# The matrix-memory layer of a small transformer: dense work spread in equal pieces, transposes one block later

## Chip, cores and metric

The kernel runs on one core of one Trainium2 chip. The metric is the time of one execution on the device, in microseconds (us). The engines are TensorE (PE, matmuls; PEld is its weight load), VectorE (DVE), ScalarE (ACT), GpSimd (POOL) and SyncE (SP, which issues the weight transfers). All data is 32-bit.

## The reference

Two blocks of two layers run on 256 latent and 256 context tokens of width 1024. Each layer has a mixer and a squared-ReLU MLP of width 4096. The change touches one mixer of the four, the "mLSTM" (matrix memory) of the second block's first layer. It has 8 heads, with queries and keys of 64 and values of 128:

```
q, k, v, o, gates = split(u @ w_in)                 # u: normed input, 512 tokens
b = cumsum(log_f);  d = b[t] - b[s] + log_i[s]      # per head and direction, masked to the scan's past
m_t = max(max_s d, inter)
wq = exp(d - m_t) * (q @ k.T)                       # decay weights times scores
h = (wq @ v + carry) / max(|sum(wq) + carry|, exp(-m_t))
hs = h_forward + flip(h_backward)
y = (rms_norm_per_head(hs) * head_norm * sigmoid(o)) @ w_out
```

The kernel writes the chunked recurrence out as one masked product per head: for every tile of 128 queries, exp(decay arguments) times the scores, for both directions, normalised, added, transposed and multiplied with the values.

## The kernel before, in words

Every large product is made of three fast passes (L646 to L648), because each 32-bit operand is split in a rounded high part and a rest: high x high, low x high, high x low. A weight tile of 128 x 2048 comes into `ring` by a transfer from SP, ACT rounds it into `w_h` (L1145, two halves), and DVE subtracts to get `w_l` (L1509, two halves). Both hold two tiles. Each engine has its own queue, written out by hand in the order of the code, and semaphores tie the queues together.

The layer's mixer is in these phases:

- `m_in`: gates, queries, keys and the first quarter of the values. Its last tile has four units, one for each 128 tokens, which DVE copies out of PSUM (L1496).
- `m_gates`: 16 small transposes on PE (L1024) turn the gate rows into columns, and DVE copies them into `tm` (L1955).
- `m_heads`: 32 blocks, b = 4 x head + query tile. In the first two query tiles of a head (latent) a block has 512 keys, in the other two (context) 256. "Long" and "short" blocks are meant by this below.
- `to_h` with `m_out`: four tiles of the output projection. Beside them DVE makes the modulation vectors of a later layer out of streamed weights (L1528, L1530), adds the results to `h` (L1899) and splits the next weights.

One block of `m_heads` goes through the engines so: POOL adds the mask to the decay rows (`args`, L2159); ACT makes the exponentials (`decay`, L1393 and L1395: four for a long block, two for a short one); PE makes the scores (`qk`, L1038); DVE multiplies the two and sums (L1990, twice, called W below), works out the reciprocal (L1995 to L1997); ACT scales the forward part with it (`scale`, L1402); DVE adds the backward part (L2010, called P); PE transposes (`turn`, L1048) into bank 5; ACT copies that out (`turned`, L1409); PE multiplies two such blocks with the values (`values`, L1064). After each head there are copy (`head_out`, L1415), squares (L2166), mean square on PE (`mean_square`, L1072), logarithm, exponent and norm (L1420, L1973, L1427, L1965), rounding (`round_out`, L1431) and rest (`rest_out`, L1580) for the output projection.

The blocks' decay arguments are in three buffers, `mbuf(b)`. `args(b)` overwrites the buffer of block b-3 and so waits until `turn(b-3)` is done. `qk` has two banks, and `qk(b)` waits for W of block b-2.

Among the blocks stands the rest of the input projection, 20 dense units of 24 passes: 12 token-major ones for the values (`tokm`, 256 columns) and 8 feature-major ones for the output gate (`fm`, 512 columns). `dense_slots` puts unit k in block 3k//2, so two blocks of three have one and every third has none. In the code of PE:

```
for b in range(n):
    if b + 2 < n:
        qk(b + 2)
    dense(b)
    turn(b)
    if b % 2 == 0 and b:
        values(b // 2 - 1)
    if b % 4 == 3 and b > 4:
        mean_square(b // 4 - 1)
```

## Time and profile before

| | |
|---|---|
| time before, median of 3 runs | 2445.49 us (2441.13 to 2446.42) |
| the profiled execution, its own time | 2443.79 us |
| its span | 2442.0 us |
| PE busy over the span | 2269.7 us (93%) |
| DVE, ACT, POOL busy | 1679.6, 885.2, 672.5 us |
| `m_heads`, first `qk` to first pass of the output projection | 1418.69 to 1628.90 us |

The profiled execution's time is 1.79 us more than its span, for what lies around the span, and 1.70 us less than the median. "Busy" counts a matmul's modelled duration, at whatever clock it ran. PEclk is TensorE's granted clock as a share of 2.4 GHz, so 0.50 is 1.2 GHz. A number in brackets behind a timeline row is the idle time of that engine before it, and who ended it; "x4" means four instructions merged.

### The profile page before, as it was taken

Reading aid. Unit: us, or ns where it says so; the run is one execution under the profiler, and the core shown is the slowest. Engines: PE = TensorE matmul, PEld = TensorE weight load, DVE = VectorE, ACT = ScalarE, POOL = GpSimd, SP = SyncE. Lnnn points to the kernel's source line nnn. Section 1 sums busy time; section 2 is a strip of 40 time slices with the busy share of each in tenths; the row PEclk is TensorE's granted clock in tenths of the full one; section 3 lists DMA queues with packets and bytes.
Section 4 is the critical chain, followed back from the end, with each engine's and each line's share of the span. In section 5 each row is a group of like instructions: output and inputs, shape, how many; then the busy total and the mean of one; then the engine's idle time right before and its main releaser. Section 6 shows DMA issues by size and latency. Waiting matters only on the chain. (4 is left out here: it accounts for less than half of the span.)

```text
span 2442.0 us, 31167 instructions
## 1 busy us (share of the span) xinstructions
PE 2269.7 (93%) x12408; PEld 1892.2 (77%) x12408; DVE 1679.6 (69%) x2431; ACT 885.2 (36%) x1357; POOL 672.5 (28%) x434
## 2 busy tenths in 40 slices
PE   5999999899999889999988888878999998898998
PEld 5887678688888678899987666656888887657997
DVE  6665658988669955767777845569876775596343
ACT  1323333222333233444433445542223334244444
POOL 3001210233345500113465022212323462002244
PEclk9999999999999989999988989889999999899999
DMA  8422124455555462356655421113655564203652
GB/s 278 153 87 74 47 87 155 138 198 181 189 190 185 141 188 77 114 162 192 216 173 161 146 82 61 52 52 132 212 179 201 190 172 97 69 1 106 189 173 86
DMA packets 268025, 341.14 MB, mean 140 GB/s; under 512 B 31056, under 2 KB 181464, under 8 KB 267624
## 3 DMA queue, kind: packets, MB, share of 16 engines
q1 hardware_dynamic: 266704, 334.92, 42.8%
q10 hardware_dynamic: 1176, 4.23, 0.5%
q8 instruction: 99, 1.62, 0.3%
q14 instruction: 46, 0.38, 0.0%
HBM read 338.04 MB, written 1.08 MB: 139 GB/s over the span
## 5 line engine op out<-in xcount | busy, mean ns | idle before, releaser
L646 PE MATMUL PS<-a_h,w_h 128*128 128x512 f32 (+1 forms) x2808 | 974.9, 347 | 43.8 <-DVE a_l L1689 28.5
L647 PE MATMUL PS<-a_l,w_h 128*128 128x512 f32 (+1 forms) x2808 | 961.8, 343 | 0.0
L648 PE MATMUL PS<-a_h,w_l 128*128 128x512 f32 (+1 forms) x2808 | 961.3, 342 | 0.0
L1509 DVE TENSOR_TENSOR w_l<-ring,w_h 128x1024 fp32r<-128x1024 f32 (+1 forms) x434 | 596.9, 1416 | 257.0 <-ACT w_h L1145 256.3
L646 PEld LDWEIGHTS PS<-a_h,w_h 128*128 128x128 f32 x2808 | 541.2, 193 | 138.0 <-issue 57.4
L1145 ACT ACTIVATE w_h<-ring 128x1024 fp32r<-128x1024 f32 (+1 forms) x434 | 426.7, 1033 | 583.1 <-PE PS L648 529.5
L648 PEld LDWEIGHTS PS<-a_h,w_l 128*128 128x128 f32 x2808 | 540.9, 193 | 59.6
L647 PEld LDWEIGHTS PS<-a_l,w_h 128*128 128x128 f32 x2808 | 541.8, 193 | 56.0
L1530 DVE SCALAR_TENSOR_TENSOR bias<-ring,silu,bias 128x512 f32<-128x512 f32 x532 | 453.3, 906 | 4.2 <-DMA ring<-in_w_mod 0.5
L2076 POOL TENSOR_TENSOR a_l<-hid,a_h 128x2048 fp32r<-128x2048 f32 (+1 forms) x60 | 228.4, 3807 | 241.6 <-ACT a_h L1161 241.6
L2091 POOL TENSOR_TENSOR hid<-hid 128x256 f32<-128x256 f32 (+1 forms) x128 | 157.7, 1233 | 414.8 <-ACT hid L1127 414.8
L1127 ACT ACTIVATE hid<-PS 128x512 f32<-128x512 f32 (+1 forms) x136 | 67.6, 498 | 382.0 <-PE PS L648 381.8
L1553 DVE TENSOR_REDUCE mod<-PS 128x4 f32<-128x512 f32 x76 | 49.5, 684 | 132.6 <-PE PS L714 132.2
L646 PE MATMUL PS<-w_h,a_h 128*128 128x256 f32 x384 | 116.8, 304 | 20.7 <-DVE a_l L1689 20.5
L2120 POOL TENSOR_TENSOR bias<-windows,aux 128x256 f32<-128x256 f32 x32 | 29.3, 938 | 311.6 <-DVE nmax L1794 163.9
L647 PE MATMUL PS<-w_l,a_h 128*128 128x256 f32 x384 | 113.2, 295 | 0.0
L648 PE MATMUL PS<-w_h,a_l 128*128 128x256 f32 x384 | 113.0, 294 | 0.0
L1127 ACT ACTIVATE big<-PS 128x256 f32<-128x256 f32 (+1 forms) x90 | 41.7, 464 | 192.0 <-PE PS L648 191.9
L646 PE MATMUL PS<-m_h,w_h 128*128 128x512 f32 (+1 forms) x320 | 108.3, 338 | 1.0 <-DVE m_l L1765 1.0
L648 PE MATMUL PS<-m_h,w_l 128*128 128x512 f32 (+1 forms) x320 | 107.5, 336 | 0.0
L647 PE MATMUL PS<-m_l,w_h 128*128 128x512 f32 (+1 forms) x320 | 107.5, 336 | 0.0
L646 PEld LDWEIGHTS PS<-w_h,a_h 128*128 128x128 f32 x384 | 78.4, 204 | 33.6 <-issue 28.8
(181 smaller groups left out, 2379.6 us busy)
## 6 DMA issues: line engine op xcount, KB each, us to landing
ring<-in_w_ff SPq DMA_DIRECT2D x64, 1024.0 KB, 5.7
ring<-in_ffn_w SPq DMA_DIRECT2D x64, 1024.0 KB, 5.5
ring<-in_w_mod SPq DMA_DIRECT2D x48, 1024.0 KB, 5.2
ring<-in_ada_w SPq DMA_DIRECT2D x48, 1024.0 KB, 5.2
ring<-in_w_in SPq DMA_DIRECT2D x42, 1024.0 KB, 5.3
ring<-in_mlstm_w_in SPq DMA_DIRECT2D x12, 1024.0 KB, 5.6
ring<-in_w_o SPq DMA_DIRECT2D x8, 1024.0 KB, 5.0
ring<-in_w_attn_out SPq DMA_DIRECT2D x4, 1024.0 KB, 5.6
```

The lines of the kernel that those rows point to most:

```text
L646: nc.tensor.matmul(out, stat[0], mov[0], start=start, stop=False, **kw)
L647: nc.tensor.matmul(out, stat[0], mov[1], start=False, stop=False, **kw)
L648: return nc.tensor.matmul(out, stat[1], mov[0], start=False, stop=stop, **kw)
L1127: nc.scalar.activation(out, PS[0:m, bank_of[u], src_cols], func, **kw).then_inc(s_free[bank_of[u]], 1)
L1145: nc.scalar.activation(w_h[:, n % 2, c], raw[:, c], ACT.Copy).then_inc(s_wh, 1)
L1509: V.tensor_tensor(w_l[:, n % 2, c], ring[:, split_raw[n] % SLOTS, c], w_h[:, n % 2, c].bitcast(F32), ALU.subtract).then_inc(s_wl, 1)
L1530: ins = V.scalar_tensor_tensor(out=acc[:, v, :], in0=w[:, k, :], scalar=sc, in1=acc[:, v, :], op0=ALU.mult, op1=ALU.add)
L1553: ins = V.tensor_reduce(sums[:, :, v], PS[:, 6 + v, :].rearrange("p (c n) -> p c n", n=P), AX_X, ALU.add)
L2076: nc.gpsimd.tensor_tensor(lo, hid[:, 4 * (g % 8):4 * (g % 8) + 4, 0:cols], hi.bitcast(F32), ALU.subtract).then_inc(s_xl, 1)
L2091: nc.gpsimd.tensor_tensor(x, x, x, ALU.mult).then_inc(s_ff, 1)
L2120: ins = nc.gpsimd.tensor_tensor(bias[:, hh % 2, c].rearrange("p (i c) -> p i c", i=4), shifted, aux[:, A_MASK + LAT * q:A_MASK + LAT * q + ...
```

## The change

The order of work of the matrix-memory layer is written anew in the queues of all engines:

- **Pieces.** A dense unit of 512 columns is cut in halves, so that there are 28 pieces: 16 halves of 12 passes and 12 token-major units of 24. `piece(b)` puts one in each block but 8, 17, 26 and 31.
- **Transposes.** PE does `turn(b-1)` at the end of its turn through the loop for block b, and so `values` and the last steps shift by one turn. ACT does `turned(b-1)` right behind `scale(b)` and ahead of `decay(b+2)`.
- **Weights.** Rounding and splitting are done by halves, one in each of two blocks. The tile that follows the seventh, `m_out`'s second, is no longer prepared in `m_heads`.
- **Gates.** The 16 transposes of the gate rows stand behind the second unit of `m_in`'s last tile, in bank 5, and DVE copies them behind its second copy.
- **Output projection.** Its first tile goes over k for both units together, and the last head's mean square stands in it, behind k = 5.

```
-            return {3 * k // 2: unit for k, unit in enumerate(units)}
+        def piece(b):
+            p = b - (b // 9)
+            return (p // 4, p % 4) if b % 9 < 8 and p < 28 else None
+        TILE_ENDS = {-1: -1, 0: 3, 1: 7, 2: 12, 3: 16, 4: 21, 5: 25}
+        def tile_to_prepare(b, since):
+            return next((i + 2 for i, end in TILE_ENDS.items() if end + since == b), None)
...
@@ PE, output projection
+                        if ph["src"] == "m" and i == 0:
+                            for ks in (range(0, 6), range(6, 8)):
+                                if ks[0]:
+                                    mean_square(MH - 1)
+                                for k in ks:
...
@@ PE, m_in
                             if i == 5:
                                 tokm(st, u + j, w, j)
+                                if j == 1:
+                                    gate_columns()
...
@@ PE, m_heads
-                    for b in range(n):
+                    for b in range(n + 1):
                         if b + 2 < n:
                             qk(b + 2)
-                        dense(b)
-                        turn(b)
-                        if b % 2 == 0 and b:
-                            values(b // 2 - 1)
+                        if b < n:
+                            dense(b)
+                        if b % 2 and b > 2:
+                            values((b - 3) // 2)
+                        if b:
+                            turn(b - 1)
                         if b % 4 == 3 and b > 4:
                             mean_square(b // 4 - 1)
                     values(2 * MH - 1)
-                    mean_square(MH - 1)
...
@@ ACT, m_heads
-                    round_w(ph["s"] + 1)
                     decay(0)
                     decay(1)
                     for b in range(n):
-                        if b % 4 == 0 and b >= 8:
-                            log_variance(b // 4 - 2)
                         scale(b)
+                        if b:
+                            turned(b - 1)
                         if b + 2 < n:
                             decay(b + 2)
...
+                        if qt == 2 and hh >= 1:
+                            head_out(hh - 1)
+                        if qt == 2 and hh >= 2:
+                            norm_and_gate(hh - 2)
+                        for i in range(2):
+                            t = tile_to_prepare(b, 1 + i)
+                            if t is not None:
+                                round_half(ph["s"] + t, i)
+                        if qt == 0 and hh >= 2:
+                            log_variance(hh - 2)
+                        if qt == 0 and hh >= 3:
+                            round_out(hh - 3)
+                        if piece(b) is not None and piece(b)[0] % 2 == 0 and piece(b)[1] % 2:
+                            output_gate(piece(b)[0], piece(b)[1] // 2)
+                    turned(n - 1)
...
@@ DVE, m_heads
                         dve.wait_ge(s_scaled, b + 1)
                         V.scalar_tensor_tensor(out=x0, in0=x1, scalar=rc[:, 1:2], in1=x0, op0=ALU.mult, op1=ALU.add
                                                ).then_inc(s_P, 1)
+                        for i in range(2):
+                            t = tile_to_prepare(b, 2 + i)
+                            if t is not None:
+                                split_half(ph["s"] + t, i)
+                        if qt == 3 and hh >= 2:
+                            normed(hh - 2)
+                        if qt == 1 and hh >= 3:
+                            rest_out(hh - 3)
```

Two places show how it moves instructions. The first is ACT's queue in the middle of `m_heads`. L1402 is `scale`, L1409 `turned`, L1393 `decay` and L1415 `head_out`. Before, from a copy of transposes on:

```order
604 L1409 ACTIVATE work<-PS 128x4x128 [waits m_pv_done,m_transposed]
605 L1402 ACTIVATE work<-work,den 128x512 [waits m_denominator_ready]
606 L1393 ACTIVATE work<-work,tm 128x256 [waits m_decay_args]
607 L1393 ACTIVATE work<-work,tm 128x256
608 L1415 ACTIVATE hid<-PS 128x512 [waits m_pv_done]
609 L1409 ACTIVATE work<-PS 128x4x128 [waits m_pv_done,m_transposed]
```

Of the change, one turn through the same loop. Here L1439 is `scale`, L1446 `turned`, L1430 and L1432 `decay`, L1452 `head_out`, L1464 the exponential of the norm and L1182 half a weight tile's rounding:

```order
663 L1439 ACTIVATE work<-work,den 128x256 [waits m_denominator_ready]
664 L1446 ACTIVATE work<-PS 128x4x128 [waits m_pv_done,m_transposed]
665 L1430 ACTIVATE work<-work,tm 128x256 [waits m_decay_args,m_decay_rows_loaded_0]
666 L1432 ACTIVATE work<-work,tm 128x256
667 L1430 ACTIVATE work<-work,tm 128x256
668 L1432 ACTIVATE work<-work,tm 128x256
669 L1203 DMA bias<-decay_rows 128x1024 [waits m_decay_args]
670 L1452 ACTIVATE hid<-PS 128x512 [waits m_pv_done]
671 L1464 ACTIVATE aux<-aux 128x512 [waits m_exponent_ready]
672 L1182 ACTIVATE w_h<-ring 128x1024 [waits unit_done,weights_loaded_0]
673 L1439 ACTIVATE work<-work,den 128x256 [waits m_denominator_ready]
```

The copy of the transposes, which stood last in a block, now stands between the block's `scale` and its `decay`, and everything else of the block stands between `decay` and the next `scale`.

The second place is PE's queue where the heads end. "windows,unit" is a mean square, "work,big" the values, "m_h,w_h" the output projection. Before, from the last transposes on:

```order
7310 L1048 MATMUL PS<-ident,work 128x128 [waits m_probsT_ready,m_probs_ready]
7311 L1048 MATMUL PS<-ident,work 128x128
7312 L1072 MATMUL PS<-windows,unit 128x512 [waits m_squares]
7313 L1064 MATMUL PS<-work,big 128x256 [waits m_probsT_ready]
7314 L1064 MATMUL PS<-work,big 128x256
7315 L1072 MATMUL PS<-windows,unit 128x512 [waits m_squares]
7316 L646 MATMUL PS<-m_h,w_h 128x512 [waits input_split,bank_evacuated_2,weights_split]
```

Of the change, the end of the 36 passes that now stand ahead of the last mean square, which is L731 here:

```order
7348 L648 MATMUL PS<-m_h,w_h 128x512
7349 L649 MATMUL PS<-m_l,w_h 128x512
7350 L650 MATMUL PS<-m_h,w_l 128x512
7351 L731 MATMUL PS<-windows,unit 128x512 [waits m_squares]
7352 L648 MATMUL PS<-m_h,w_h 128x512 [waits input_split]
```

The last mean square has moved from the front of the output projection to behind six of eight k of its first tile.

## Rows read from the trace of the kernel before

**Rows 1.** Busy us of PE, PEld, DVE, ACT, POOL, then granted clock, in two stretches.

```profile
1418.00:1629.00 211.00, 173.18 (x753) 125.50 (x753) 113.89 (x307) 110.21 (x220) 51.17 (x40) 0.85 0.15 50
1633.00:1679.00 46.00, 42.04 (x194) 34.81 (x193) 44.71 (x62) 8.07 (x9) 17.18 (x13) 1.00 0.53 173
```

**Rows 2.** Waits from 1418 to 1629 us: who, for whom, total, times, longest.

```profile
PE PS L1048 <- DVE work L2010: 31.7, 10, 5.9
```

**Rows 3.** Timeline of PE alone, blocks 5 and 6, at full clock.

```profile
1460.16 0.60 PE L1048 MATMUL PS<-ident,work 128*128 128x128 f32 x4
1460.60 1.03 PE L1064 MATMUL PS<-work,big 128*128 128x256 f32 x4
1461.56 0.70 PE L1038 MATMUL PS<-big 64*128 64x256 f32 x2
...
1463.52 1.12 PE L1038 MATMUL PS<-big 64*128 64x512 f32 x2
...
1464.58 0.39 PE L646 MATMUL PS<-w_h,a_h 128*128 128x256 f32 x1
...
1467.56 0.38 PE L1048 MATMUL PS<-ident,work 128*128 128x128 f32 x2
1467.78 1.89 PE L1064 MATMUL PS<-work,big 128*128 128x256 f32 x8
```

**Rows 4.** Timeline of POOL, ACT and DVE at the same place.

```profile
1460.85 1.27 POOL L2159 TENSOR_TENSOR work<-bias,aux 128x512 f32<-128x512 f32 x1 [2.85 <-PE PS L1048]
1461.29 0.71 ACT L1402 ACTIVATE work<-work,den 128x512 f32<-128x512 f32 x1
1462.04 0.75 DVE L2010 SCALAR_TENSOR_TENSOR work<-work,den 128x512 f32<-128x512 f32 x1 [1.25 <-ACT work L1402]
1462.15 0.91 ACT L1393 ACTIVATE work<-work,tm 128x256 f32<-128x256 f32 x2
1462.71 0.41 DVE L1990 CUSTOM_DVE_ANT_0 work<-work,PS 128x256 f32<-128x256 f32 x1
```

**Rows 5.** Groups by line and shape, 1418 to 1629 us: count, busy, mean ns, idle.

```profile
L1509 DVE TENSOR_TENSOR w_l<-ring,w_h 128x1024 fp32r<-128x1024 f32 x16 | 20.6, 1329 | 26.4 <-ACT w_h L1145 26.3
L1145 ACT ACTIVATE w_h<-ring 128x1024 fp32r<-128x1024 f32 x15 | 15.0, 1046 | 0.0
```

**Rows 6.** Granted clock (third from the right) in short stretches.

```profile
1464.00:1468.00 4.00, 4.00 (x30) 3.40 (x29) 3.00 (x11) 2.27 (x7) 1.92 (x2) 1.00 0.33 128
1504.00:1508.00 4.00, 4.00 (x19) 3.82 (x19) 2.46 (x8) 1.40 (x3) 0.00 (x0) 0.50 0.24 94
1316.00:1318.00 2.00, 2.00 (x11) 2.00 (x11) 1.97 (x4) 0.00 (x0) 2.00 (x1) 0.50 0.97 333
```

**Rows 7.** Timeline of PE: waits that ended shortly before those stretches.

```profile
1501.65 0.44 PE L1048 MATMUL PS<-ident,work 128*128 128x128 f32 x2 [3.54 <-DVE work L2010]
1314.28 1.42 PE L714 MATMUL PS<-ident,bias 128*128 128x128 f32 x8 [2.10 <-DVE bias L1530]
```

**Rows 8.** Timeline where the heads begin.

```profile
1416.43 1.15 PE L1024 MATMUL PS<-ident,work 8*128 8x8 f32 x16
1422.85 0.69 DVE L1990 CUSTOM_DVE_ANT_0 work<-work,PS 128x512 f32<-128x512 f32 x1 [0.74 <-ACT work L1395]
1424.21 1.22 PE L1038 MATMUL PS<-big 64*128 64x256 f32 x2 [3.57 <-DVE den L1990]
```

**Rows 9.** Timeline where they end and the output projection begins.

```profile
1623.36 0.63 PE L1048 MATMUL PS<-ident,work 128*128 128x128 f32 x2
1628.35 1.12 PE L1072 MATMUL PS<-windows,unit 128*128 128x512 f32 x2 [1.80 <-POOL windows L2166]
1633.08 0.69 DVE L1580 TENSOR_TENSOR m_l<-hid,m_h 128x512 fp32r<-128x512 f32 x1 [0.70 <-ACT m_h L1431]
1640.43 0.88 DVE L1899 SCALAR_TENSOR_TENSOR h<-PS,mod,h 128x256 f32<-128x256 f32 x2 [1.11 <-PE PS L648]
1651.11 1.03 PE L714 MATMUL PS<-ident,bias 128*128 128x128 f32 x8
```

More of the change, by code:

```diff
@@ L1006, in _, with gate_columns @@
                 elif kind == "m_in":
+                    def gate_columns():
+                        pe.wait_ge(s_gr, 1)
+                        out = PS[:, 5, :].rearrange("p (w t g n) -> p w t g n", w=2, t=4, g=2, n=32)
+                        for what in range(2):
+                            for d in range(2):
+                                src = G[:, 2 * d + 1, :] if what == 0 else Bc[:, d, :]
+                                for tt in range(4):
+                                    mm = nc.tensor.transpose(out[:, what, tt, d, 0:MH], src[:, P * tt:P * tt + P],
+                                                             ident[0:MH, 0:MH])
+                        mm.then_inc(s_cols, 1)
                     first_tile(ph["steps"][0], ph["x"] - KC, False, gate_view)
@@ L1067, in values @@
                         mm.then_inc(s_mpv, 1)
[L1069 to L1073 removed]
                     def dense(b):
[L1077 removed]
+                        if piece(b) is None:
                             return
[L1079 removed]
+                        i, q = piece(b)
                         st = ph["steps"][i]
@@ L1939, in scan_rows, with gate_columns @@
                             step(ins)
+                    def gate_columns():
+                        dve.wait_ge(s_cols, 1)
+                        src = PS[:, 5, :].rearrange("p (w t g n) -> p w t g n", w=2, t=4, g=2, n=32)
+                        for what in range(2):
+                            for d in range(2):
+                                ins = V.tensor_scalar(tm[:, what, :, :, d], src[:, what, :, d, 0:MH],
+                                                      -1.0 if what == 0 else 1.0, None, ALU.mult)
+                        ins.then_inc(s_tm, 1)
                     for i, st, u in steps_of(ph):
@@ L1948, in _ @@
                             copy_unit(u + j, mv[:, j, 0:256], slice(0, 256))
-                elif kind == "m_gates":
-                    wait_units(dve, u)
-                    dve.wait_ge(s_unit, u + 1)
-                    src = PS[:, bank_of[u], :].rearrange("p (w t g n) -> p w t g n", w=2, t=4, g=2, n=32)
-                    for what in range(2):
-                        for d in range(2):
-                            ins = V.tensor_scalar(tm[:, what, :, :, d], src[:, what, :, d, 0:MH],
-                                                  -1.0 if what == 0 else 1.0, None, ALU.mult)
-                            if not (what and d):
-                                step(ins)
-                    ins.then_inc(s_free[bank_of[u]], 1)
+                            if j == 1:
+                                gate_columns()
                 elif kind == "m_heads":
```

108 lines of the change are left out of this document (52 added, 56 removed).

## The prediction

> **What bounds the kernel now.** I read the page first (PE is busy 93% of the span), then the busy time by stretches, then the waits of the one stretch that the change rewrites. From 1418 to 1629 us PE is busy 173 of 211 us at a mean granted clock of 0.85 [rows 1]. DVE and ACT are busy little over half of it, so neither is the bound by its sum. PE's waits are nearly all of one kind: ten of them, 31.7 us, in which the transposes (L1048) wait for P, DVE's last step of a block [rows 2]. They fall in the blocks without a dense unit. The reader should see two costs there: the wait, and the clock behind it. After 3.54 us of waiting PE ran at 0.50 for the next stretch, which is the 1.2 GHz level; after a wait of 2.10 us elsewhere it did too; in the busy blocks 5 and 6 it ran at 1.00 [rows 6, 7].
>
> How large is each? I price PE's work at full clock, start to start [rows 3]: long scores 1.06 (1463.52 to 1464.58), short ones about 0.63 (0.70 less the overlap that the long ones show); transposes 0.44 and 0.22; values 0.96 and about 1.82; a token-major unit 2.98; a mean square about 1.0, as two passes of 512 columns like the long scores. 96 passes of 512 columns took 22.2 us (1628.90 to 1651.11) [rows 9], so half a feature-major unit is 2.8. From the third score to the last transposes that is 80 us of dense work (12 x 2.98 + 16 x 2.8), 25 of scores (14 long, 16 short), 10 of transposes, 21 of values and 7 of mean squares (the last of either comes after): 143. From the third score (1424.21, [rows 8]) to the end of the last transposes (1623.36 + 0.22, [rows 9]) are 199.4 us. Take off 143 and 31.7: some 24 us went to the low clock.
>
> The second part is the output projection. From 1633 to 1679 DVE is busy 44.7 of 46 us [rows 1]: DVE is the bound there, and its chain starts when the last head's rest is done (1633.08 + 0.69 [rows 9]).
>
> **The change part by part.**
>
> *The dense pieces.* They remove no work from PE. They take the ten waits' cause away: from the score of block b+2 (which waits for W of block b) to the transposes of block b there are only the reciprocal, `scale` and P, some 2.9 us, and a piece of 2.8 to 3.0 now covers it in 28 of 32 blocks.
>
> *The transposes one block later.* They need no wait for P at all. But `args(b+2)` must wait for `turn(b-1)`, now at the end of PE's turn b, where before it was one turn earlier. And on ACT `decay(b+2)` stands ahead of `scale(b+1)`. So a loop closes over two turns. From the end of `turn(b-1)` [rows 3, 4]: POOL starts 0.25 later and takes 1.27, `decay(b+2)` starts 0.03 behind it (1462.12, 1462.15) and takes 0.8 (two exponentials, 0.91 with their overlap) or 1.6 (four); `scale(b+1)` to P 0.75 (1461.29, 1462.04); P to the next W 0.67 (1462.04, 1462.71); W to the score that it releases 1.36 for a long block [rows 8]. For short blocks I take 0.55, 0.45 and 0.8, in the ratio of P's and W's column counts. That gives L = 4.6, 4.2, 5.5 and 6.0 us for b in query tile 0, 1, 2, 3. Queued inside this loop is all that ACT has between `decay` and the next `scale`, and DVE between P and the next W: half a rounding 1.0, half a split 1.2 (means 1046 and 1329 ns [rows 5], the latter with some blocked ones), an output gate 1.15 (two operations), and four ACT and two DVE operations of 512 columns in each head at 0.55 to 0.8 (nearest rows 0.71 and 0.75 [rows 4]). L with these is 4.2 to 9.5, on the mean 6.9.
>
> PE's own turn C is 3.6, 5.0, 4.4 and 7.0 for the four tiles of a head (the last has the long values and the mean square), 1 to 2 where the piece is missing. The end T of turn b is the later of T(b-1) and T(b-2) + L(b-2), plus C(b). Put down block by block this gives 47 us at block 8, 99 at 16, 147 at 24 and 185 at the last transposes: 143 of work and 42 of waits. L exceeds the C that should hide it, 6.9 against 4.5, so PE waits about 2.4 us in every second block. So at full clock the body is 185 against 175 before: the spread removes 32 us of waits and the late transposes bring 42.
>
> *The clock.* This cost no row shows for the new pattern. Bounds: none (185), and the loss of the widest fall of before, where behind the 3.54 us wait half clock reached to about 1508, for each of nine waits of 2 us or more (about 215, part of it absorbed by the next wait). Before, eight falls cost 24 us, 3 each. Of the new waits nine or ten reach 2 us; a longer turn of PE shortens the next wait, which gives part back. I take 17: body 202, +2.6 us against 199.4.
>
> *The gate transposes.* The 1.15 us [rows 8] move ahead of two dense units, as does the copy into `tm`. The mask additions and exponentials of blocks 0 to 2 then run beside dense work, and W of block 0 waits for its own score alone. The last unit ends 1.15 later, at about 1417.6; copy 0.4, score 1.0, W at 1419.5, the third score at 1420.9 against 1424.21: -3.3 us. Range -2 to -5. The rounding of the second weight tile was ahead of `decay(0)`; it now comes behind and its first use is in block 4.
>
> *The last mean square.* Squares were ready 4.8 us after the last transposes (1628.35 less 1623.58 [rows 9]). In the new order PE starts 36 passes of the output projection about 2.2 us behind the last transposes; they take 36 x 0.231 = 8.3, so the mean square starts at 10.5, not at 4.8: the last rest, 5.4 us behind it (1628.35 to 1633.77 [rows 9]), is 5.7 us later. PE gains 8 us of passes that nobody waits for, since the bound there is DVE. Queued behind the rest on DVE are the modulation vectors, then, new, both halves of the second weight tile's split, 2.3 us, then the additions to `h`. Before, DVE waited 1.1 us for PE at that place [rows 9]; that goes. Sum +5.7 + 2.3 - 1.1 = +6.9, less if ACT's shorter queue brings the squares earlier and PE starts later: I take +6.6, bounds +3 and +9. Transfers keep their cover, since SP sends four tiles ahead and DMA was busy 15% of this part [rows 1].
>
> *Sum.* +2.6 - 3.3 + 6.6 = +5.9 us on the profiled execution's 2443.79: 2449.7. The median is 1.7 above that execution, so 2451.
>
> **Rivals.**
>
> A. The clock stays up. Nothing here shows a drop behind a wait of 0.6 us (block 6 ran at 1.00 [rows 6]), and the real waits may be more even than mine, each of 1 to 1.5 us. Then the body is 185 to 190 and the sum 2443.8 - 12 - 3.3 + 6.6 = 2435, 2437 from the median. This is the case on the other side. It decides where the body falls below about 191 us. Against it speaks the fall behind 2.10 us [rows 6, 7].
>
> B. The clock falls for longer, as behind the 3.54 us wait, behind each longer wait: body about 210, sum +14: 2459.
>
> C. The parts cancel: body at 198, or the last rest is only 3 us late. Then the kernel is within 3 us of before, 2446.
>
> D. POOL and DVE block each other inside the loop. DVE's split of 1024 columns has a mean of 1329 ns over 16 [rows 5]; how much of that is blocking no row of these says alone. If every `args` met an operation of DVE of 0.75 (P [rows 4]), half of the 32 loops would carry it: 16 x 0.75 = 12 us more, 2463. For it: in the new order splits follow P directly, when `args` of the same turn runs. Against: with 114 us of DVE in 211 a meeting is no rule. The Trainium skill (SBUF — State Buffer, section "SBUF: two separate sides") says that VectorE operations with two SBUF inputs and GpSimd share a port pair as an exclusive lock, held for the whole instruction; by it every such meeting costs the loser its full wait, which is this rival at its worst.
>
> On the clock the Trainium skill (TensorE: Matmul & The Clock Gate, section "A second HAM failure mode: psum-queue depth-cycling") says that frequent short idles between groups of matmuls make the clock swing and cost more than the idle itself. Rows 6 and 7 agree for waits of 2.10 and 3.54 us; for shorter ones nothing here shows it. By that rule the forecast or B holds and not A.
>
> **How the numbers follow.** Forecast 0.40 (2451, own range 2445 to 2459); A 0.25 (2437); B 0.15 (2459); C 0.13 (2446); D 0.07 (2463). About 0.2%, 4.9 us, is what a measurement of this kernel can tell from no change: 2440.6 to 2450.4. Faster: A and a little of the rest, 0.27. Same: C and the lower third of the forecast, 0.26. Slower 0.47. The range is 2434 to 2463, which leaves out the far ends of A and of B and D.
>
> **What the profile of the changed kernel would show.** PE's waits should have moved from the transposes to the scores (waiting for L1990's successor), some 35 to 42 us in sum, mostly in every second block; transposes should wait for nothing. POOL's `args` should start 0.25 us behind each `turn`, and `scale` directly behind `decay` and its followers. From the third score to the last transposes 195 to 210 us; below 191 A is right. The first `args` should start near 1413. The last mean square should start 10 us behind the last transposes, and DVE should be busy without a gap behind the last rest. Granted clock over the heads 0.80 to 0.90; at 0.95 or more the clock term is wrong, and with it the sign.

## The result, and the profile of the changed kernel

The changed kernel takes 2462.32 us (median of 4 runs, 2457.75 to 2463.10), the kernel before 2443.86 (4 runs, 2441.13 to 2446.42). The ratio is 1.0072, 95% interval 1.0054 to 1.0090: slower, by 17.6 us at the ratio's middle. The forecast was 2451 with a range of 2434 to 2463.

The page of the changed kernel, its span and busy times (the time of this execution is 2462.24 us):

```profile
span 2460.3 us, 31162 instructions
PE 2283.4 (93%) x12408; PEld 1902.4 (77%) x12408; DVE 1676.3 (68%) x2431; ACT 887.3 (36%) x1357; POOL 683.7 (28%) x434
```

The number of matmuls is that of before. PE is "busy" for 13.7 us more. A matmul counts for longer at the low clock, but the mean granted clock of the span differs little, 0.958 against 0.960, and these sums don't say where the 13.7 us arise.

The waits from 1421 to 1640 us (who, for whom, total, times, longest):

```profile
POOL work L2209 <- PE PS L1075: 147.5, 29, 14.1
DVE work L2052 <- ACT work L1439: 86.8, 29, 9.1
ACT work L1446 <- PE PS L1075: 73.5, 25, 6.6
PE PS L1065 <- DVE den L2037: 38.8, 17, 4.2
ACT work L1430 <- POOL work L2209: 28.3, 27, 2.0
```

Where [rows 2] had PE waiting at the transposes, it now waits at the scores (L1065) for W (L2037), 38.8 us against 31.7. The other rows are the same loop seen from each engine: POOL waits for the transposes, ACT for POOL, DVE for ACT, PE for DVE. When every engine waits for the next one, no engine is the bound: the loop is.

One round of it, from the timeline of all engines (a bracket is the idle time before the row, and who ended it; rows in between are left out, marked or not). L1075 is a pair of transposes, L2209 the mask addition, L1430 the exponentials, L1439 `scale`, L2052 P, L2037 W and L1065 the score; L1182 and L1556 are half a weight tile's rounding and split:

```profile
1611.47 0.38 PE L1075 MATMUL PS<-ident,work 128*128 128x128 f32 x2
1611.93 1.27 POOL L2209 TENSOR_TENSOR work<-bias,aux 128x512 f32<-128x512 f32 x1 [5.48 <-PE PS L1075]
1613.23 0.51 ACT L1430 ACTIVATE work<-work,tm 128x256 f32<-128x256 f32 x1 [0.96 <-POOL work L2209]
...
1614.85 1.04 ACT L1182 ACTIVATE w_h<-ring 128x1024 fp32r<-128x1024 f32 x1
1615.80 0.71 ACT L1439 ACTIVATE work<-work,den 128x512 f32<-128x512 f32 x1
...
1616.18 0.38 PE L1075 MATMUL PS<-ident,work 128*128 128x128 f32 x2
1616.54 0.75 DVE L2052 SCALAR_TENSOR_TENSOR work<-work,den 128x512 f32<-128x512 f32 x1 [5.22 <-ACT work L1439]
1616.64 1.77 POOL L2209 TENSOR_TENSOR work<-bias,aux 128x512 f32<-128x512 f32 x1 [3.44 <-PE PS L1075]
1617.21 2.29 DVE L1556 TENSOR_TENSOR w_l<-ring,w_h 128x1024 fp32r<-128x1024 f32 x1
1619.42 0.68 DVE L2037 CUSTOM_DVE_ANT_0 work<-work,PS 128x512 f32<-128x512 f32 x1
1620.77 1.22 PE L1065 MATMUL PS<-big 64*128 64x256 f32 x2 [4.20 <-DVE den L2037]
```

Follow it, start to start: PE is done with the transposes at 1611.69, where its next row starts, the decay arguments (POOL) start 0.24 later and take 1.30, the four exponentials 1.62, half a rounding (L1182) 0.95, `scale` (L1439) 0.74, P (L2052) 0.67, half a split (L1556) 2.21, W 1.35, and the score starts at 1620.77, 9.1 us behind the transposes. PE's own work in that time ended with the next transposes, at 1616.57, so it waited 4.20 us. A rounding and a split that nobody waits for at that moment are 3.2 of the 9.1.

Behind each such wait stands the clock. First the third score to the last transposes as a whole, then the stretches behind the wait of 3.90 us that ended at 1482.48 (the granted clock is the third number from the right), and that wait:

```profile
1424.75:1635.72 210.97, 172.20 (x742) 126.39 (x742) 103.64 (x295) 104.71 (x205) 49.22 (x36) 0.85 0.15 50
1483.00:1485.00 2.00, 2.00 (x5) 1.16 (x4) 1.90 (x4) 0.73 (x2) 0.00 (x0) 0.50 0.00 0
1485.00:1489.00 4.00, 4.00 (x16) 3.17 (x15) 1.86 (x8) 0.00 (x0) 0.00 (x0) 0.76 0.02 4
1489.00:1493.00 4.00, 4.00 (x18) 2.63 (x16) 0.00 (x0) 2.77 (x5) 1.27 (x1) 1.00 0.00 0
```

```profile
1482.48 1.22 PE L1065 MATMUL PS<-big 64*128 64x256 f32 x2 [3.90 <-DVE den L2037]
```

After the wait PE runs at 0.50, the 1.2 GHz level, and is back by 1489. In windows of 1 us over the whole stretch I count 11 such falls, 61.4 us at half clock; before there were 8, with 56.3.

Where the heads begin and end, as in [rows 8, 9]: first the gate transposes, the copy into `tm`, the first `args` and the third score, then the last transposes, the last mean square, the last rest and the stretch of DVE behind it.

```profile
1414.47 1.15 PE L1039 MATMUL PS<-ident,work 8*128 8x8 f32 x16
1415.65 0.48 DVE L1994 TENSOR_SCALAR tm<-PS 128x32 f32<-128x32 f32 x4 [0.65 <-PE PS L1039]
1416.22 3.79 POOL L2209 TENSOR_TENSOR work<-work,aux 128x512 f32<-128x512 f32 x3 [71.91 <-DVE tm L1994]
1424.75 0.70 PE L1065 MATMUL PS<-big 64*128 64x256 f32 x2 [0.69 <-DVE den L2037]
```

```profile
1635.44 0.44 PE L1075 MATMUL PS<-ident,work 128*128 128x128 f32 x2
...
1645.53 1.02 PE L731 MATMUL PS<-windows,unit 128*128 128x512 f32 x2
...
1650.15 0.69 DVE L1627 TENSOR_TENSOR m_l<-hid,m_h 128x512 fp32r<-128x512 f32 x1 [0.70 <-ACT m_h L1468]
...
1655.52 2.35 DVE L1548 TENSOR_TENSOR w_l<-ring,w_h 128x1024 fp32r<-128x1024 f32 x2
1657.79 1.65 DVE L1946 SCALAR_TENSOR_TENSOR h<-PS,mod,h 128x256 f32<-128x256 f32 x4
...
1670.56 1.27 DVE L1600 TENSOR_REDUCE mod<-PS 128x4 f32<-128x512 f32 x2
```

**The bill.** Four times divide the profiled executions: the last modulation reduction on DVE ahead of the heads (1405.03 before, 1408.82 after), the third score, the end of the last transposes, and the first modulation reduction behind them (1652.19, 1670.56). The differences are +3.8 up to the first, -3.25 from there to the third score, +11.4 to the last transposes (199.6 to 211.0) and +6.4 in the tail (28.4 to 34.8). (The end is that of the second of the last transposes, 0.2 us behind the one that the prediction's 199.4 takes.) They add up to 18.3, the difference of the spans. The +3.8 arises where no instruction of the change stands. The nine kernels below have that code unchanged too, and there this time lies between 1403.4 and 1408.9; it differs from run to run, and how much of it is in the medians stays open.

Of the 11.4 us in the heads, 0.95 is work that moved. PE's loop now does the seventh head's mean square ahead of the last transposes, where before it stood behind them, so there are seven in this stretch and before there were six (one takes 0.95 us, from 1611.69 to the next row of PE at 1612.64).

### The profile page after: what moved, and what is told of

It is laid out like the page before. It is cut to its first block, busy times and chain, and to the rows that moved or that the text cites. A ratio compares the mean times of both kernels' runs of the same rounds, so it can differ in the third digit from the quotient of the medians.

```text
span 2460.3 us, 31162 instructions
## 1 busy us (share of the span) xinstructions
PE 2283.4 (93%) x12408; PEld 1902.4 (77%) x12408; DVE 1676.3 (68%) x2431; ACT 887.3 (36%) x1357; POOL 683.7 (28%) x434
## 3 DMA queue, kind: packets, MB, share of 16 engines
q10 hardware_dynamic: 1176, 4.23, 0.5%
q8 instruction: 99, 1.62, 0.3%
## 4 chain that ended last, share of the span: by engine, by line
PE 76%; DVE 14%; ACT 3%; issue 3%; POOL 3%; DMA 1%; SPq 0%; ACTq 0%; POOLq 0%; DVEq 0%
PE PS L648 22%; PE PS L649 21%; PE PS L650 21%; DVE bias L1577 4%; DVE w_l L1548 2%; PE PS L889 2%; PE PS L912 2%; PE PS L716 1%; DVE work L1722 1%; DVE a_l L1736 1%; PE PS L899 1%; PE PS L1065 1%; POOL a_l L2126 1%; PE PS L844 1%; POOL work L2209 1%
## 5 line engine op out<-in xcount | busy, mean ns | idle before, releaser
L1548 DVE TENSOR_TENSOR w_l<-ring,w_h 128x1024 fp32r<-128x1024 f32 (+1 forms) x420 | 578.8, 1419 | 233.0 <-ACT w_h L1174 232.3
L1174 ACT ACTIVATE w_h<-ring 128x1024 fp32r<-128x1024 f32 (+1 forms) x420 | 413.2, 1034 | 572.1 <-PE PS L650 520.4
L2141 POOL TENSOR_TENSOR hid<-hid 128x256 f32<-128x256 f32 (+1 forms) x128 | 165.9, 1298 | 405.0 <-ACT hid L1156 405.0
```

The costliest lines, as they stand in the source:

```text
L1174: nc.scalar.activation(w_h[:, n % 2, c], raw[:, c], ACT.Copy).then_inc(s_wh, 1)
L1548: V.tensor_tensor(w_l[:, n % 2, c], ring[:, split_raw[n] % SLOTS, c], w_h[:, n % 2, c].bitcast(F32), ALU.subtract).then_inc(s_wl, 1)
L2141: nc.gpsimd.tensor_tensor(x, x, x, ALU.mult).then_inc(s_ff, 1)
```

## The experiments

Every kernel has 4 or 5 runs; e1 to e4 stand against 9 runs of the kernel before on their chip (median 2442.93), e5 to e7 against 8 (2441.22), e8 and e9 against 9 (2442.39). The table gives the places of the bill, worked out from each trace: "start" from the reduction to the third score, "body" from there to the end of the last transposes, PE's waits in the body (sum, how many of 2 us or more), the falls of the clock there (count, us at half clock), the remainder of the body when its waits and 143 us of work are taken off, and the tail. Not all of the remainder is clock. In e2, with no fall, it is 2.3 us, so six mean squares and all else are 145.4 us of work. The kernels with the late transposes (all but before, e2, e5 and e8) have the seventh mean square there too, which makes 3.3. In e6 the first piece of 12 passes, 2.8 us, stands ahead of the third score and so outside of the body.

| kernel | median us | start | body | waits (2 us or more) | falls, us low | remainder | tail |
|---|---|---|---|---|---|---|---|
| before | 2443.86 | 19.18 | 199.6 | 31.7 (7) | 8, 56.3 | 24.9 | 28.4 |
| changed | 2462.32 | 15.93 | 211.0 | 38.8 (8) | 11, 61.4 | 29.2 | 34.8 |
| e1_four | 2404.37 | 15.92 | 153.2 | 5.6 (0) | 1, 3.4 | 4.6 | 34.9 |
| e2_same_block | 2398.41 | 15.93 | 148.9 | 3.5 (0) | 0 | 2.3 | 34.9 |
| e3_tail | 2454.15 | 15.93 | 209.3 | 38.7 (8) | 10, 54.6 | 27.6 | 31.0 |
| e4_extras | 2430.65 | 15.92 | 180.2 | 23.0 (5) | 5, 23.9 | 14.2 | 36.0 |
| e5_best | 2395.01 | 15.92 | 148.9 | 3.5 (0) | 0 | 2.4 | 31.6 |
| e6_dense_first | 2413.68 | 18.11 | 161.3 | 16.1 (1) | 1, 3.4 | 2.2 | 35.8 |
| e7_four_only | 2432.86 | 15.93 | 185.8 | 25.0 (6) | 7, 30.7 | 17.8 | 34.8 |
| e8_unit_order | 2397.14 | 15.93 | 148.9 | 3.6 (0) | 0 | 2.3 | 31.2 |
| e9_shift_only | 2474.95 | 19.18 | 227.6 | 54.5 (9) | 11, 82.8 | 30.2 | 27.4 |

A saving "under the changed kernel" below is the difference of two medians that were taken beside different sets of runs of the kernel before; these sets differ by up to 2.6 us in the medians.

The theory is the loop: transposes, decay arguments, exponentials, `scale`, P, W, score, over two turns. Its rivals are that the pieces do the harm (dense work in every block gets in the way), that the tail makes the loss, and that POOL and DVE block each other. The first group takes the loop apart.

**e1_four.** A fourth buffer for the decay arguments, and ACT's copy of the transposes last in its turn, so that both reach one turn further.

```
-  return (scr[:, 0, :, :], scr[:, 1, :, :], work[:, 4, :]...)[b % 3]
+  return (scr[:, 0, :, :], scr[:, 1, :, :], work[:, 4, :]..., fourth[:, :, :])[b % 4]
...
                         scale(b)
-                        if b:
-                            turned(b - 1)
                         if b + 2 < n:
                             decay(b + 2)
...
+                        if b:
+                            turned(b - 1)
...
-                        if b >= 3:
-                            pool.wait_ge(s_mt, b - 2)
+                        if b >= 4:
+                            pool.wait_ge(s_mt, b - 3)
```

> The changed kernel with a fourth buffer for decay arguments, so that args(b) waits for turn(b-4) and not turn(b-3); ACT copies the transposes (turned(b-1)) at the end of its turn b, behind decay(b+2) and all else; the squares share one buffer to make the room. Nothing is left out. Theory of the two-turn loop (late transposes free the buffer late, and decay(b+2) keeps scale(b+1) back): the loop is cut, what is left from the transposes to the next score is 0.7 + 0.75 + 0.67 + 1.36 = 3.5 us, below PE's 4.5 a turn, so the long waits of PE go: third score to last transposes 150 to 165 us against 211, total 45 to 60 us less, near 2405 to 2415. Rival, that the chain from P to W on DVE or the pieces themselves hold PE back whatever the buffers: the stretch stays above 200 us and the total within 10 us of the change.

Measured: 2404.37 us (2400.56 to 2406.99), ratio 0.9841 (0.9827 to 0.9854), 58 us under the changed kernel. PE's waits for W, in this kernel's numbering and from 1420 to 1570 us:

```profile
PE PS L1066 <- DVE den L2038: 4.9, 6, 1.3
```

Against 38.8 us in 17 waits. The pieces and the late transposes are all still there; so neither does the harm by itself. It is in what they release: the ring of buffers and, with it, the place of ACT's copy, which this run moved too (e7 tells the two apart).

**e2_same_block.** The other way to open the loop: the transposes back in their own block, on PE and on ACT, with the pieces, the gates and the tail of the change kept.

```
-                        if b % 2 and b > 2:
-                            values((b - 3) // 2)
-                        if b:
-                            turn(b - 1)
+                        turn(b)
+                        if b % 2 == 0 and b:
+                            values(b // 2 - 1)
...
                         scale(b)
-                        if b:
-                            turned(b - 1)
...
+                        turned(b)
```

> The changed kernel with the transposes back in their own block (turn(b) behind dense(b), values and mean squares as before, turned(b) last in ACT's turn); the 28 pieces, halves of weights, early gates and the new tail stay. Theory of the two-turn loop: the late transposes cost and the spreading gains; the piece covers most of the time to P, short waits of 0.5 to 1 us are left, clock near full: third score to last transposes 165 to 180 us, total 30 to 45 us under the change and 12 to 28 under the kernel before. Rival, the spreading in pieces is what costs (or the clock falls with any pattern of short waits): stretch 200 us or more, total not under the kernel before.

Measured: 2398.41 us (2397.02 to 2399.62), ratio 0.9817 (0.9804 to 0.9831). The gain over the changed kernel is 64 us where 30 to 45 were expected: I had left waits of 0.5 to 1 us and some low clock in the body, and there are 3.5 us of waits in all and no fall. The body in one row, and PE's waits in it:

```profile
1419.58:1568.44 148.86, 145.33 (x741) 107.35 (x742) 106.06 (x295) 103.43 (x205) 44.14 (x36) 1.00 0.22 71
```

```profile
PE PS L1075 <- DVE work L2048: 2.3, 4, 0.7
```

PE is busy 145 of 149 us and the clock never falls. The same instructions and one mean square more took 211 us in the changed kernel.

**e9_shift_only.** The counterpart: the kernel before with the late transposes alone, on PE and ACT.

```
-                        turn(b)
-                        if b % 2 == 0 and b:
-                            values(b // 2 - 1)
+                        if b % 2 and b > 2:
+                            values((b - 3) // 2)
+                        if b:
+                            turn(b - 1)
...
                         scale(b)
+                        if b:
+                            turned(b - 1)
...
-                        turned(b)
```

> The kernel before with the transposes one block later on PE (values with them) and ACT's copy ahead of decay(b+2), and nothing else: whole dense units in two blocks of three, gates and tail as before. Theory of the two-turn loop: the late transposes alone cost. Waits move from the transposes to the scores and grow from 32 to some 50 us, since a whole unit covers the loop only in every second turn and leaves the next bare; with 20 to 30 us of low clock, third score to last transposes 215 to 230 us against 200, total 15 to 30 us over the kernel before. Rival, with whole units (5.6 us) the loop is covered and the shift costs nothing there: total within 5 us of before.

Measured: 2474.95 us (2473.97 to 2477.49), ratio 1.0130 (1.0116 to 1.0144). Body and waits hit, the total is 33 us over before where at most 30 was expected. With it the four corners are there (body, us):

| | transposes in their block | one block later |
|---|---|---|
| units in two blocks of three | 199.6 (before) | 227.6 (e9) |
| pieces in 28 of 32 | 148.9 (e2) | 211.0 (changed) |

The pieces are worth 51 us with the transposes in their block and 17 with the late ones. The late transposes cost 28 and 62, of which 0.95 each is the moved mean square. The lower row holds more than the pieces: halves of weight tiles, the early gate transposes and ACT's and DVE's order of the other steps are in it as well, and no run takes them apart. That the pieces remove the very waits that had hidden part of the loop is my reading of these four numbers; no run shows it by itself.

**e7_four_only.** The fourth buffer of e1 without its change of ACT's order.

```
-  return (scr[:, 0, :, :], scr[:, 1, :, :], work[:, 4, :]...)[b % 3]
+  return (scr[:, 0, :, :], scr[:, 1, :, :], work[:, 4, :]..., fourth[:, :, :])[b % 4]
...
-                        if b >= 3:
-                            pool.wait_ge(s_mt, b - 2)
+                        if b >= 4:
+                            pool.wait_ge(s_mt, b - 3)
```

> The changed kernel with the fourth buffer but ACT's order of the change (scale, turned(b-1), decay(b+2), the rest). Theory: the mask addition (1.3 us) leaves the loop, the copy of the transposes (0.7) takes its place, decay and ACT's other work stay in it: L falls by 0.85, about 14 us of waits over 16 loops and 8 to 12 of clock, third score to last transposes 185 to 192, total 20 to 28 less than the change. Rival, the buffer alone is what holds: as good as the run with the fourth buffer and ACT's copy last (153 us), total near 2404.

Measured: 2432.86 us (2430.40 to 2435.72), ratio 0.9967 (0.9953 to 0.9981); waits 25.0 us, 13.8 less, and the body 185.8. That is 29 us under the changed kernel, a little more than the 20 to 28 expected. POOL now waits for transposes of one turn further back, but ACT's `turned(b-1)` stands ahead of `decay(b+2)` and waits for the same transposes, in this kernel's waits from 1419 to 1606 us:

```profile
ACT work L1447 <- PE PS L1076: 76.3, 28, 6.0
```

So the loop was closed at two places, by a buffer and by the order of a queue. Opening the first gives 29 us, both 58; ACT's order alone, with three buffers, was not run.

**e4_extras.** ACT's order of the change, but with all that isn't part of the loop (copies, rounding, gate, norm) ahead of `turned` and `decay` rather than behind them, where ACT waits anyway.

```
                         scale(b)
-                        if b:
-                            turned(b - 1)
-                        if b + 2 < n:
-                            decay(b + 2)
                         if qt == 2 and hh >= 1:
                             head_out(hh - 1)
...
+                        if b:
+                            turned(b - 1)
+                        if b + 2 < n:
+                            decay(b + 2)
```

> The changed kernel with ACT's other work of a turn (head_out, norm, halves of weights, logarithm, round_out, output gate) ahead of turned(b-1) and decay(b+2), so that it lies in ACT's wait for the transposes and no longer between decay(b+2) and scale(b+1). Same instructions. Theory of the two-turn loop: the loop loses ACT's 1.2 us on the mean, in 16 loops about 19 us, some of it lost again where the other chain binds: third score to last transposes 190 to 200 against 211, total 10 to 20 us less. Rival, PE's waits are set elsewhere (POOL, DVE, clock): within 3 us of the change.

Measured: 2430.65 us (2428.81 to 2430.99), ratio 0.9947 (0.9933 to 0.9961), 32 us under the changed kernel where at most 20 was expected, and the body is 180.2 where 190 to 200 was. The waits fell by 15.8 us, and the remainder by another 15.0, which is the clock, since I had not coupled the one to the other.

**e6_dense_first.** The change with `dense(b)` ahead of `qk(b+2)`, so that the dense piece runs while W is made.

```
                     for b in range(n + 1):
-                        if b + 2 < n:
-                            qk(b + 2)
                         if b < n:
                             dense(b)
+                        if b + 2 < n:
+                            qk(b + 2)
```

> The changed kernel with one swap on PE: dense(b) ahead of the score of block b+2. Three buffers, transposes one block later and ACT's order stay. Theory of the two-turn loop: its length from the transposes to the score is unchanged, but now a piece of 2.8 to 3.0 us lies in the wait, so the loop closes in L + C - 2.9: third score to last transposes 150 to 170 us against 211, no waits of 2 us left but where a piece is missing, total 40 to 60 us less than the change. Rival, the loop's length itself bounds the heads (the 16 loops would have to take 211 us wherever PE's piece lies): total within 10 us of the change.

Measured: 2413.68 us (2412.35 to 2416.99), ratio 0.9887 (0.9873 to 0.9902). Its waits, and a stretch with two of them in it:

```profile
PE PS L1065 <- DVE den L2037: 15.4, 15, 3.2
```

```profile
1475.62 1.12 PE L1065 MATMUL PS<-big 64*128 64x512 f32 x2 [0.81 <-DVE den L2037]
```

```profile
1466.00:1486.00 20.00, 19.19 (x92) 13.97 (x92) 13.25 (x37) 12.60 (x27) 7.52 (x5) 1.00 0.28 79
```

Fifteen waits remain, but of 1.0 us on the mean, and the clock stays at 1.00 through them. It fell once, behind the single wait of 3.16 us. Here 22.7 us of waits less brought 49.7 us of body. Of the rest 2.8 are the piece that moved out of the body, and 24.2 the clock: it gave as much as the waits.

**e3_tail.** The last mean square back ahead of the output projection.

```
-                            for ks in (range(0, 6), range(6, 8)):
-                                if ks[0]:
-                                    mean_square(MH - 1)
+                            mean_square(MH - 1)
+                            for ks in (range(0, 8),):
```

> The changed kernel with the last head's mean square ahead of the output projection's first tile again; the tile still goes over k for both units, and the second tile is still split in the projection. Theory (the mean square stands behind 36 passes and with it the last rest, where DVE is the bound): the last mean square starts about 5 us and not 10 behind the last transposes, the projection ends 4 to 6 us earlier, total 4 to 6 less than the change. Rival, the tail's 6.3 us come from the second tile's split and from the end of the heads: total within 1.5 us of the change.

Measured: 2454.15 us (2453.51 to 2455.07), ratio 1.0046 (1.0034 to 1.0059). The median is 8.2 us under the changed kernel's where 4 to 6 was expected, by the two ratios 6.4. The edit accounts for less: the tail is 3.8 us shorter, just under what was expected. Another 3.65 arise ahead of the heads (the reduction is at 1405.17 against 1408.82) and 1.7 in the body, both of which this edit leaves alone. So much, some 4 us, two profiled executions can differ by where the code is the same. The mean square and the last rest:

```profile
1635.33 2.05 PE L731 MATMUL PS<-windows,unit 128*128 128x512 f32 x2 [3.15 <-POOL windows L2215]
```

```profile
1640.98 0.69 DVE L1626 TENSOR_TENSOR m_l<-hid,m_h 128x512 fp32r<-128x512 f32 x1 [0.70 <-ACT m_h L1467]
```

The last rest now starts 10.6 us behind the last transposes (14.4 in the changed kernel, 9.25 before). Of the 1.3 us that are left, 0.9 is the mean square itself, 2.05 us instead of 1.12: behind this wait of 3.15 the granted clock was 0.65 from 1634 to 1638, while in the kernel before the wait there was 1.80 [rows 9] and the granted clock from 1629 to 1641 us 1.00.

**e5_best and e8_unit_order.** e5 is e2 with the mean square first, and with the second weight tile rounded and split at the heads' end rather than in the projection; e8 is e5 with the output projection unit by unit too, so that of the change's tail only the place of that rounding and split is left. Before they stood earlier, some 12 us ahead of the last transposes (the rounding at 1610.60, the split at 1611.68).

```
+                            mean_square(MH - 1)
+                            for ks in (range(0, 8),):
...
+                        if b == n - 1:
+                            round_half(ph["s"] + 8, 0)
                         turned(b)
+                        if b == n - 1:
+                            round_half(ph["s"] + 8, 1)
...
+                    for i in range(2):
+                        split_half(ph["s"] + 8, i)
                     rest_out(MH - 2)
```

And e8 against e5:

```
-                        if ph["src"] == "m" and i == 0:
-                            mean_square(MH - 1)
-                            for ks in (range(0, 8),):
...
                     values(2 * MH - 1)
+                    mean_square(MH - 1)
```

> The transposes in their own block, the last mean square ahead of the output projection, and the projection's second weight tile rounded and split at the end of the heads (ACT around the last copy of transposes, DVE behind the last but one norm), where DVE waits; pieces and early gates stay. Theory (the tail's +6.3 us are 3.8 for the late mean square and about 2.5 for the second tile's split): from the last transposes to the first modulation sum 29 us against 34.9 with both and 31.0 with the mean square alone put back, body as in the run with the transposes in their own block, 149 us; total 5 to 6 us under that run, near 2393. Rival, with the heads short the tail is bound by something else: total within 1.5 us of that run, or the rounding delays the last head and it is slower.

> As the run with the second tile split at the end of the heads, but the output projection's first tile goes unit by unit again (unit 0 over all k, then unit 1), the last mean square ahead of it. So the tail is that of the kernel before but for the place of the second tile's split. Theory: what was left of the tail is the order over k, which ends both units late and lets DVE wait 2.1 us for PE at its first additions to h; this run's tail is 29 to 30 us from the last transposes to the first modulation sum (31.6 with the order over k, 28.4 before), total 1.5 to 3 us under that run, near 2393. Rival, the rounding and split at the heads' end delay the last head and cost what they save: tail 31 or more, total the same.

Measured: e5 2395.01 us (2394.18 to 2399.92), ratio 0.9813 (0.9798 to 0.9828); e8 2397.14 us (2394.27 to 2397.66), ratio 0.9808 (0.9795 to 0.9822). Their intervals overlap with e2's: the 3.3 us that the profiled tail is shorter lie within what the medians can tell. Both expectations missed: for e5 5 to 6 us under e2 were expected with a tail of 29, and it is 3.4 with 31.6; for e8 another 1.5 to 3 with 29 to 30, and it is nothing with 31.2, as its rival said. In both the tail is some 3 us longer than before, so the order over k is not the reason. DVE in e5, then PE's wait at the last mean square, ACT's second half of the rounding, and the granted clock behind the wait:

```profile
1574.62 3.19 DVE L1555 TENSOR_TENSOR w_l<-ring,w_h 128x1024 fp32r<-128x1024 f32 x2
...
1581.17 0.69 DVE L1626 TENSOR_TENSOR m_l<-hid,m_h 128x512 fp32r<-128x512 f32 x1 [0.70 <-ACT m_h L1465]
...
1588.70 1.66 DVE L1945 SCALAR_TENSOR_TENSOR h<-PS,mod,h 128x256 f32<-128x256 f32 x4 [2.07 <-PE PS L650]
```

```profile
1575.74 1.09 PE L731 MATMUL PS<-windows,unit 128*128 128x512 f32 x2 [3.98 <-POOL windows L2217]
1570.36 1.05 ACT L1179 ACTIVATE w_h<-ring 128x1024 fp32r<-128x1024 f32 x1
1577.00:1580.00 3.00, 3.00 (x9) 2.31 (x8) 2.30 (x4) 1.20 (x2) 0.00 (x0) 0.50 0.00 0
```

The split left the projection (2.35 us in the changed kernel), but there DVE now waits 2.07 us for PE, and the last rest starts 11.3 us behind the last transposes. The second half of ACT's rounding (1570.36) stands ahead of the last head's steps, and the mean square comes 5.86 us behind the last transposes instead of 4.52 before and 4.91 in e3. DVE's split, 3.19 us from 1574.62 on, then keeps the last head's step on DVE waiting. The 2.07 us come at least in part from the clock: the wait for the mean square is now 3.98 us where it was 1.80 before, and behind it PE ran at 0.50 in the projection's first passes, where before it ran at 1.00. So what is saved behind the rest is lost in front of it and at PE. This is read from rows; no run changed the rounding's place alone.

## Why the prediction was right in its sign and off in its size

The sign, the loop and three of four terms stood; the forecast was +5.9 us and 17.6 were measured (18.3 between the profiled executions). The measured 2462.32 is 0.7 us below the end of the range. With the clock's term wrong, and 3 us of the 17.6 outside of the change's places, that it lies inside is owed to the width of the range. The forecast also added 1.7 us to come from the profiled execution to the median; with its fourth run the median before is 2443.86, and +5.9 on it would be 2450. Point by point:

- **What bounds the kernel.** Right. The dense pieces take away the waits of before, and the clock behind them: e2 shows 3.5 us of waits and no fall. The work that I priced at 143 us was 145.4 there (148.9 less 3.5). I had put seven mean squares in it for both kernels; before had six in this stretch and the change has seven.
- **The loop over two turns.** Right, place and size. The round shown above took 9.1 us, within my L of 4.2 to 9.5; I forecast 42 us of waits, at the scores, and 38.8 were there, with no row for transposes. e1 and e7 show its two closures.
- **The clock.** This is the step that failed. I took 17 where before had 24.7 by the same reckoning, because "a longer turn of PE shortens the next wait, which gives part back". It gave nothing back: the remainder is 29.2. Against before, waits made +7.1 (forecast +10.3), the moved mean square +0.95 (forecast nothing) and the clock +3.3 (forecast -7.7), so the body grew by 11.4 instead of 2.6. A fall costs 2.35 us (29.2 less 3.3 of work, over 11), somewhat less than before (24.9 less 2.3, over 8: 2.8). I had nine or ten waits that reach 2 us; there were eight such waits and eleven falls, eight of them at waits of 3.02 to 4.23 us, one where the heads begin, one behind a wait of 1.58, one behind 1.15 and 1.28 close together. Had I priced ten falls like those before, 3 each, the sum would have been 2464. The stretch took 211.0 us, just above the 195 to 210 that I had said the profile would show.
- **The start.** Forecast -3.3, measured -3.25. The first `args` start at 1416.22, which is 1412.4 without the 3.8 us that came up earlier; I had said near 1413.
- **The tail.** Forecast +6.6, measured +6.4. The mean square starts 9.8 us behind the last transposes (10.5 forecast) and the last rest 5.2 later than before (5.7 forecast); behind the rest are 1.3 more (2.3 of split less the 1.1 of waiting, as forecast). e3 gives 3.8 of it back.
- **Rivals.** A (the clock stays up, body 185 to 190) did not come in the changed kernel; e6 shows the case that it described, waits of 1 us at full clock. B (the clock falls for longer, body about 210, 2459) gave the body that was measured, but not by its mechanism: the falls were not longer than before, there were more of them. C fell with the body. D (POOL and DVE block each other) exists but is small: the 29 `args` have a mean of 1.445 us against about 1.28 in e2, which is 5 us in sum, all of it in the loop at most, where I had 12; so its 2463, the number closest to the measured one, is a coincidence.

```profile
L2209 POOL TENSOR_TENSOR work<-bias,aux 128x512 f32<-128x512 f32 x16 | 23.1, 1445 | 85.2 <-PE PS L1075 85.2
```

```profile
L2205 POOL TENSOR_TENSOR work<-bias,aux 128x512 f32<-128x512 f32 x16 | 20.4, 1274 | 43.5 <-PE PS L1075 43.5
```

The first is the changed kernel's group from 1421 to 1640 us, the second e2's from 1416 to 1570 (mean ns behind the busy time).

The 3.0 us between the sum of the change's places (14.6) and the measured 17.6 are not explained by any of them; they are of the size of the 3.8 ahead of the heads.

## What to carry to other kernels

When work is shifted one turn later, look for what it releases: a ring of three buffers that had covered the loop was one short after the shift, and every in-order queue that waits for the shifted work closes the same loop again (here ACT's), so that opening one place gives only part. Work that nobody waits for belongs ahead of the instruction at which an engine idles anyway (e4: 32 us for a change of order alone). And price a long wait of PE with the fall of the clock behind it: in e1, e2, e4, e6 and e7 every microsecond of waiting taken away brought 0.7 to 1.1 more of the clock.

## What the runs showed that I had not expected

- **Short waits are nearly free of the clock.** In e6 fifteen waits of 1.0 us on the mean left it at 1.00 but for one fall behind 3.16 us. In the changed kernel waits of 1.48, 1.10, 1.12 and 1.24 us had no fall behind them, 1.58 had one. All eight of 3.02 us and more had one. Between the two the length alone doesn't decide: in e7 a wait of 2.10 us had a fall and one of 2.61 had none:

```profile
1538.60 0.70 PE L1066 MATMUL PS<-big 64*128 64x256 f32 x2 [2.61 <-DVE den L2038]
1539.00:1542.00 3.00, 3.00 (x14) 2.31 (x13) 2.18 (x7) 0.72 (x1) 0.00 (x0) 1.00 0.28 95
```

The Trainium skill (TensorE: Matmul & The Clock Gate, section "A second HAM failure mode: psum-queue depth-cycling") says that frequent short idles between groups of matmuls make the clock swing, and that this costs throughput on top of the idle. For 3 us and more the traces agree, for 1 us those of e6 do not.
- **DVE and POOL slow each other where they meet.** In the round above the split (1617.21 to 1619.50) took 2.29 us and the arguments beside it (1616.64 to 1618.41) 1.77, against 1.27 for the arguments one turn earlier and 1.17 to 1.18 for each half in the pair of L1548 (2.35 for two). The Trainium skill (SBUF — State Buffer, section "SBUF: two separate sides") describes a port pair that VectorE and GpSimd share as an exclusive lock. The rows fit it: the arguments start 0.10 us behind P (1616.54) and lose 0.50, about what P still has to run, and the split starts behind the arguments and loses 1.1, about what they still have to run. No run takes the meeting away, and the means over all blocks show that such meetings are few.
- **The best of these kernels are 1.9% under before**, e2, e5 and e8 at 2395 to 2398 us: the pieces, the weights by halves and the early gate transposes, without the late transposes. Seen from e2, the change held a gain of 45 us and, in the late transposes, a loss of 64.
